# Hyena convolution: forward transform, spectral product and inverse transform in one phase

## The reference

```python
def long_conv_bidir(z, h_fwd, h_bwd):
    n = z.shape[1]
    nfft = 2 * n
    zf = jnp.fft.rfft(z.astype(jnp.float32), n=nfft, axis=1)
    hf = jnp.fft.rfft(h_fwd, n=nfft, axis=0) + jnp.conj(jnp.fft.rfft(h_bwd, n=nfft, axis=0))
    return jnp.fft.irfft(zf * hf[None], n=nfft, axis=1)[:, :n]

def hyena_branch(u, conv_w, conv_b, ...):
    x0, x1, v = jnp.split(short_conv(u, conv_w, conv_b), 3, axis=-1)
    z = x1 * v
    ...
    y = long_conv_bidir(z, h_fwd, h_bwd).astype(u.dtype) + z * skip
    return x0 * y
```

## Time and profile before

| what | value |
|---|---|
| median of 3 runs | 4414.9 us (4414.67 to 4422.24) |
| the profiled execution, its own time | 4423.86 us |
| its span in the trace | 4422.0 us |
| mean granted TensorE clock | 0.956 |
| TensorE busy | 3986.4 us (90%) |
| VectorE busy | 1482.3 us (34%) |
| ScalarE busy | 1015.8 us (23%) |

### The profile page before, as it was taken

How to read it: one execution, slowest core, us unless ns; L and a number is a source line. 1 busy time by engine, 2 the same in 40 slices (tenths; PEclk the granted TensorE clock), 3 DMA queues, 4 the chain that set the end, 5 groups by cost and what they waited for, 6 DMA issues and landing times. The chain is left out here.

```text
span 4422.0 us, 95422 instructions
## 1 busy us (share of the span) xinstructions
PE 3986.4 (90%) x41485; PEld 2616.3 (59%) x41485; DVE 1482.3 (34%) x2542; ACT 1015.8 (23%) x2416; POOL 606.4 (14%) x732
## 2 busy tenths in 40 slices
PE   7898799998999969999978999989999989997995
PEld 2343345885444458888854444459888944445774
DVE  2556321123212220000033666555666532222002
ACT  2200100022101112222233442034444311112433
POOL 1030000001110000000010001234555311000112
PEclk8899899999999979999989999989999999997998
DMA  6361211102111169999971001100000021124998
GB/s 218 114 206 63 109 45 67 38 10 53 50 33 60 65 234 393 398 401 395 393 270 41 7 5 43 39 6 4 4 3 4 4 89 49 51 91 182 389 383 317
DMA packets 233137, 588.67 MB, mean 133 GB/s; under 512 B 36424, under 2 KB 140776, under 8 KB 213193
## 3 DMA queue, kind: packets, MB, share of 16 engines
q1 hardware_dynamic: 192159, 462.92, 28.7%
q0 software_dynamic: 19120, 73.68, 4.8%
q10 hardware_dynamic: 21626, 48.70, 3.2%
HBM read 514.20 MB, written 71.05 MB: 132 GB/s over the span
## 5 line engine op out<-in xcount | busy, mean ns | idle before, releaser
L1646 PE MATMUL experts_bank<-experts_uT,ex_wu 128*64 128x96 f32 x9216 | 391.1, 247 | 26.9 <-PE experts_bank L1632 22.2
L1646 PEld LDWEIGHTS experts_bank<-experts_uT,ex_wu 128*64 128x64 f32 x9216 | 384.7, 138 | 43.6 <-issue 43.6
L1719 DVE TENSOR_TENSOR experts_hT<-experts_si,experts_bank 128x384 f32<-128x384 f32 (+1 forms) x68 | 31.3, 460 | 724.3 <-PE experts_bank L1646 724.3
L192 PE MATMUL vgproj_bank<-vg_w,mix_hT 128*128 128x256 f32 x1024 | 225.8, 383 | 11.1 <-DVEq L201 7.6
L192 PEld LDWEIGHTS vgproj_bank<-vg_w,mix_hT 128*128 128x128 f32 x1024 | 195.8, 192 | 41.5 <-DVEq L201 8.4
L1646 PE MATMUL experts_bank<-experts_uT,b2z_hT 128*64 128x96 f32 x4096 | 177.6, 248 | 27.3 <-DMA b2z_hT<-in_w 16.9
L1646 PEld LDWEIGHTS experts_bank<-experts_uT,b2z_hT 128*64 128x64 f32 x4096 | 172.1, 138 | 42.0 <-issue 42.0
L1632 PE MATMUL experts_bank<-mixed_T,experts_hT 128*32 128x256 f32 (+1 forms) x2592 | 193.9, 451 | 0.0
L2243 POOL TENSOR_TENSOR b2z_hT<-b2z_hT,rwkv_level 128x256 f32<-128x256 f32 x192 | 153.8, 834 | 159.4 <-DVE b2z_hT L2596 159.3
L2612 DVE TENSOR_TENSOR rc_xy<-rc_xy,rc_bank 128x256 f32<-128x256 f32 x288 | 120.7, 421 | 122.3 <-PE rc_bank L2257 116.6
L1632 PEld LDWEIGHTS experts_bank<-mixed_T,experts_hT 128*32 128x32 f32 x2592 | 110.4, 110 | 69.6 <-issue 0.2
(11 more groups left out here) (572 smaller groups left out, 7202.7 us busy)
## 6 DMA issues: line engine op xcount, KB each, us to landing
ex_wu<-in_expert_w SPq DMA_DIRECT2D x72, 2048.0 KB, 16.6
mixed_T<-in_expert_w SPq DMA_DIRECT2D x36, 2048.0 KB, 17.6
b2z_hT<-in_w SPq DMA_DIRECT2D x64, 1024.0 KB
b2z_Z<-in_w SPq DMA_DIRECT2D x32, 1024.0 KB, 13.6
keep_rows<-mix_hyT ACTq DMA_DIRECT2D x27, 768.0 KB, 8.9
keep_rows<-experts_yo ACTq DMA_DIRECT2D x68, 288.0 KB, 9.8
mix_hT<-in_ada_w POOLq DMA_DIRECT2D x8, 2048.0 KB, 10.0
merge_w<-in_w_in SPq DMA_DIRECT2D x32, 512.0 KB, 5.8
```

The source lines that it names most:

```text
L192: last = pe.matmul(bk[t][:, 0:width], xT[:, k, t * P:(t + 1) * P], wt[:, s, k, :], start=(k == 0), stop=(k == KT - 1))
L1646: last = pe.matmul(bk[2 + j][c:c + 64, h * BT:(h + 1) * BT], wu[:, s, j, k, h * P + c:h * P + c + 64], uT[:, s, k, :], start=(k == 0), sto ...
```

## The change

phase_forward and phase_inverse become one phase, phase_convolve. The forward part and the products stay instruction for instruction; two of the product's waits count differently (the semaphore turned takes one of the steps that chain counted, so chain counts four in a group).

The inverse matmuls are put into another order. Behind the forward matmuls TensorE issues, for par 0, the terms of the groups 0 to 2 (24 matmuls, first the four channel tiles of a = 0, then those of a = 1), which need only the first three products; then, when the fourth product is done, the last 8 terms of par 0; then par 1 as before, bank by bank. The inverse tables have no memory of their own any more: each comes as two halves of 1 MB. Those of par 0 go to the two halves of tab when the last two forward groups have been read from them, those of par 1 go to z and t when the fourth product is done. odd serves as the buffer of the closing VectorE instructions.

```diff
@@ -951,38 +951,71 @@
                     dve.tensor_tensor(H[:, kt, 3, :], odd[:, t % 2, :], even[:, :], ALU.subtract).then_inc(outs, 1)
 
 
-def phase_forward(nc, name, I, cos_in, sin_in, H, prod=None, y=None):
-
-
-    with Mem(nc, name) as m:
+def phase_convolve(nc, I, K, zn, H, prod, xc, hyT):
+
+
+    with Mem(nc, "conv") as m:
         tab = m.sb("tab", [P, 2, 16, P])
         odd = m.sb("odd", [P, 2, C])
-        z = m.sb("z", [P, 4, C]) if prod is not None else None
-        t = m.sb("t", [P, 4, C]) if prod is not None else None
+        z = m.sb("z", [P, 4, C])
+        t = m.sb("t", [P, 4, C])
+        y = hyT[:, :, 0:C]
+        back = [[tab[:, a, :, :].rearrange("p (k b) n -> p k (b n)", b=4) for a in range(2)], [z[:, :, :], t[:, :, :]]]
         bk = m.banks(8)
         full = m.sems("full0", "full1")
-        mm, free, copied, outs, chain = m.sems("mm", "free", "copied", "outs", "chain")
+        bfull = [m.sems("bfull00", "bfull01"), m.sems("bfull10", "bfull11")]
+        mm, copied, outs, chain, turned, bmm, skipped = m.sems("mm", "copied", "outs", "chain", "turned", "bmm", "skipped")
         b = m.block()
+        multiplied = lambda kt: 4 * (kt + 1)
 
         @b.sync
         def _(sp):
+            table = lambda par, a: I["k_inv"][par].rearrange("p (a n) -> p a n", n=C)[:, 4 * a:4 * a + 4, :]
             for kt in range(4):
                 if kt >= 2:
                     sp.wait_ge(mm, 4 * (kt - 1))
                 sp.dma_start(tab[:, kt % 2, :, :], I["k_fwd"][kt].rearrange("p (a n) -> p a n", n=P)).then_inc(full[kt % 2], 16)
+            for a in range(2):
+                sp.wait_ge(mm, 4 * (3 + a))
+                sp.dma_start(back[0][a], table(0, a)).then_inc(bfull[0][a], 16)
+            sp.wait_ge(chain, multiplied(3))
+            for a in range(2):
+                sp.dma_start(back[1][a], table(1, a)).then_inc(bfull[1][a], 16)
 
         @b.tensor
         def _(pe):
+
+            def inverse(par, c, a, kt, first, last):
+
+                return pe.matmul(bk[4 * par + c][:, :], prod[:, kt, 2 * par + a, c * P:(c + 1) * P], back[par][a][:, kt, :], start=first, stop=last)
+
             for kt in range(4):
                 pe.wait_ge(full[kt % 2], 16 * (kt // 2 + 1))
                 if kt >= 2:
                     pe.wait_ge(outs, kt - 1)
                 for a in range(4):
-                    src = cos_in if a < 2 else sin_in
                     for mt in range(4):
-                        last = pe.matmul(bk[kt % 2 * 4 + a][:, :], tab[:, kt % 2, a * 4 + mt, :], src[:, (a % 2) * 4 + mt, :],
+                        last = pe.matmul(bk[kt % 2 * 4 + a][:, :], tab[:, kt % 2, a * 4 + mt, :], zn[:, (a % 2) * 4 + mt, :],
                                          start=(mt == 0), stop=(mt == 3))
                     last.then_inc(mm, 1)
+            pe.wait_ge(outs, 3)
+            pe.wait_ge(chain, multiplied(2))
+            for a in range(2):
+                pe.wait_ge(bfull[0][a], 16)
+                for c in range(4):
+                    for kt in range(3):
+                        inverse(0, c, a, kt, a == 0 and kt == 0, False)
+            pe.wait_ge(chain, multiplied(3))
+            for c in range(4):
+                inverse(0, c, 0, 3, False, False)
+                inverse(0, c, 1, 3, False, True).then_inc(bmm, 1)
+            for a in range(2):
+                pe.wait_ge(bfull[1][a], 16)
+            pe.wait_ge(outs, 4)
+            for c in range(4):
+                for n in range(8):
+                    last = inverse(1, c, n // 4, n % 4, n == 0, n == 7)
+                last.then_inc(bmm, 1)
 
         @b.scalar
         def _(act):
@@ -997,15 +1030,12 @@
         def _(dve):
             then = Chain(dve, chain)
             for kt in range(4):
-                dst = [H[:, kt, n, :] for n in range(4)] if prod is None else [z[:, n, :] for n in range(4)]
                 dve.wait_ge(copied, 2 * kt + 2)
                 e = [bk[kt % 2 * 4], bk[kt % 2 * 4 + 2]]
-                dve.tensor_tensor(dst[0], e[0][:, :], odd[:, 0, :], ALU.add)
-                dve.tensor_tensor(dst[1], e[0][:, :], odd[:, 0, :], ALU.subtract)
-                dve.tensor_tensor(dst[2], odd[:, 1, :], e[1][:, :], ALU.add)
-                dve.tensor_tensor(dst[3], odd[:, 1, :], e[1][:, :], ALU.subtract).then_inc(outs, 1)
-                if prod is None:
-                    continue
+                dve.tensor_tensor(z[:, 0, :], e[0][:, :], odd[:, 0, :], ALU.add)
+                dve.tensor_tensor(z[:, 1, :], e[0][:, :], odd[:, 0, :], ALU.subtract)
+                dve.tensor_tensor(z[:, 2, :], odd[:, 1, :], e[1][:, :], ALU.add)
+                dve.tensor_tensor(z[:, 3, :], odd[:, 1, :], e[1][:, :], ALU.subtract).then_inc(outs, 1)
                 dve.wait_ge(outs, kt + 1)
                 h = [H[:, kt, n, :] for n in range(4)]
 
@@ -1015,12 +1045,25 @@
                     dve.tensor_tensor(t[:, 2, :], z[:, j, :], h[2 + j], ALU.mult)
                     then(dve.tensor_tensor(t[:, 3, :], z[:, 2 + j, :], h[j], ALU.mult))
                     dve.tensor_tensor(y[:, j, :], t[:, 0, :], t[:, 1, :], ALU.subtract)
-                    then(dve.tensor_tensor(y[:, 2 + j, :], t[:, 2, :], t[:, 3, :], ALU.add))
+                    last = dve.tensor_tensor(y[:, 2 + j, :], t[:, 2, :], t[:, 3, :], ALU.add)
+                    if j == 0:
+                        last.then_inc(turned, 1)
+                        dve.wait_ge(turned, kt + 1)
+                then(last)
 
                 dve.tensor_tensor(prod[:, kt, 0, :], y[:, 0, :], y[:, 1, :], ALU.add)
                 dve.tensor_tensor(prod[:, kt, 1, :], y[:, 2, :], y[:, 3, :], ALU.subtract)
                 dve.tensor_tensor(prod[:, kt, 2, :], y[:, 0, :], y[:, 1, :], ALU.subtract)
                 then(dve.tensor_tensor(prod[:, kt, 3, :], y[:, 2, :], y[:, 3, :], ALU.add))
+            split = lambda ap, par: ap.rearrange("p (n two) -> p two n", two=2)[:, par, :]
+            for par in range(2):
+                for c in range(4):
+                    n = par * 4 + c
+                    dve.wait_ge(bmm, n + 1)
+                    dve.scalar_tensor_tensor(odd[:, n % 2, :], split(xc[:, 4 + c, :], par), vec(K.cols, "hy_skip", c),
+                                             bk[n][:, :], ALU.mult, ALU.add).then_inc(skipped, 1)
+                    dve.wait_ge(skipped, n + 1)
+                    dve.tensor_tensor(split(hyT[:, c, :], par), odd[:, n % 2, :], split(xc[:, c, :], par), ALU.mult)
 
 
 def phase_hyena_turn(nc, K, xc, zn):
@@ -1046,45 +1089,6 @@
                     for c in range(4):
                         src = xc[:, 4 + c, :].rearrange("p (n two) -> p two n", two=2)[:, par, mt * P:(mt + 1) * P]
                         pe.transpose(bk[par * 4 + mt][:, c * P:(c + 1) * P], src, K.ident[:, :]).then_inc(tr, 1)
-
-
-def phase_inverse(nc, I, K, prod, xc, hyT):
...
 BIG = 1e30
@@ -3205,8 +3209,7 @@
         phase_taps(nc, "hin", w_in[:, :, 3072:4608], hT, K.X, xc, 6, lambda j, t: taps[j](t), col(b0), clear)
         zn = xc[:, 8:12, :].rearrange("p a (b c) -> p (a b) c", c=C)
         phase_hyena_turn(nc, K, xc, zn)
-        phase_forward(nc, "fwdz", I, zn, zn, H, prod, hyT[:, :, 0:C])
-        phase_inverse(nc, I, K, prod, xc, hyT)
+        phase_convolve(nc, I, K, zn, H, prod, xc, hyT)
 
 
 def moe(nc, tag, I, K, S, T, w_out, mixedT, wu, spare, mix_gate, hidden, scale, shift, run_cols, names, gate=None, ahead=None):
```

## The result

| | before | after |
|---|---|---|
| median | 4418.57 us (4 runs, 4414.67 to 4423.69) | 4395.61 us (4 runs, 4389.26 to 4400.4) |
| ratio to before, 95% interval | | 0.9945 (0.9933 to 0.9957) |
| profiled execution, its span | 4423.86, 4422.0 us | 4396.28, 4394.5 us |
| granted TensorE clock, mean | 0.956 | 0.958 |

The kernel is 0.55% faster; the forecast was 0.54% (4391.0, range 4386 to 4400). A ratio of 0.9945 on 4418.57 is 24.3 us; its interval, 0.9933 to 0.9957, is 19.0 to 29.6 us.

The account below looks back on a forecast made before the run. TensorE, busy 3986.4 of 4422.0 us, and its holes were taken as the bound. Forward end to inverse end falls from 79.01 to 54.93 + 0.2 = 55.13 us, saving 23.9: 4414.9 - 23.9 = 4391.0 us, range 4386 to 4400.

Parts of the forecast that it names:

- The three terms of the 24 us: Between forward and inverse transform: fourth product, barrier with table transfer, and low clock all vanish, saving 23.6 to 24.1 us.
- The marks set for the profile after: Signs expected in the new trace: no TensorE hole from 448 to 503, clock 1.00, next stage's first DMA at 505.9.
- The late weight load, 0.2 us: At TensorE's first inverse matmul, just after the third product: 0.2 us charged, bounds nothing to 0.5 us.
- The low clock, 2.0 to 2.2 us: At the old inverse's start, after TensorE's 21.9 us pause: 2.0 to 2.2 us lost, gone without a pause.
- The cover of 7.2 us: 24 inverse terms keep TensorE busy to 468.8; VectorE's fourth product is done 7.2 us before it is asked for.
- Charging nothing for the product beside a full TensorE: VectorE's fourth product beside inverse matmuls: same 0.68 to 0.69 us an instruction as beside an idle TensorE, no cost.
- The tables: SP's four 1 MB inverse table loads all hidden; margin 3 to 5 us for the second, at least 0.9 later.
- Rival B: Second table half lands 13.1 us after issue, TensorE stands: 3 to 5.4 us more, 4394 to 4396.5; chance 0.05.
- Rival C: TensorE still waits for the fourth product before the inverse: only 8.4 us saved, 4406.5; chance 0.03.
- Rival D: Short runs per bank in the inverse bring TensorE's low clock: slower, up to 4445.9 us; chance 0.02.
- Rival E: The following stage's first loads or a pause give back 3 to 16 us: 4394 to 4407; chance 0.06.

Follow-up runs that it names:

- e1: Changed kernel, but TensorE waits for the fourth product before its first inverse term, tables still early: 4409.32 us, ratio 0.9974 to the kernel before.
- e3: Changed kernel with TensorE waiting for the fourth product, and 15 useless matmuls filling that wait: 4411.78 us, ratio 0.9977 to the kernel before.
- e8: Changed kernel with par 0's second table half held back until the fourth product's second multiplication step: 4398.07 us, one execution.
- e5: Changed kernel with 18 useless VectorE instructions more in the fourth product: 4410.33 us, one execution.
- e2: Changed kernel in its new order, but par 0's two table halves asked for only after the fourth product: 4415.0 us, ratio 0.9984 to the kernel before.
- e4: Changed kernel with 8 useless VectorE instructions more in the fourth product: 4400.09 us, one execution.
- e6: Changed kernel with the loops of the first 24 inverse terms exchanged, another bank with every term: 4400.83 us, one execution.
- e7: Changed kernel with the first two forward tables loaded already in the phase before: 4392.63 us, ratio 0.9941 to the kernel before.
- e9: The changed kernel unedited, run once more on the chip of the early forward tables version: 4397.48 us, ratio 0.9947 to the kernel before.

## Why the prediction was right

- *The three terms of the 24 us.* The hole of 21.9 us and the low clock behind it were to vanish, 23.6 to 24.1 us together. The stage lost 24.00. The parts can be told apart by the experiments: waiting for the product costs 13.57 of pause (e1), the barrier and the transfer are the other 21.91 - 13.57 = 8.3 (by subtraction; no run puts back the barrier alone), and the low clock is separate from both (e3). The marks set for the profile after were met too, once the stage's later start of 1.6 us is taken off: the fourth product ended at 463.26 (461.6 forecast), the third table load was issued at 463.28 (461.7), the next phase's first load at 507.39 (505.9).
- *The late weight load, 0.2 us.* It was sized too high. The third product ends at 449.52, 0.27 us before the forward group's 449.79, and the first inverse group starts at 449.63 with no idle time. The whole inverse took 504.80 - 449.79 = 55.0 us against 54.93 + 0.2. Late weight loads can therefore have cost 0.1 us at most.
- *The low clock, 2.0 to 2.2 us.* Right for the kernel before. It isn't a constant: behind other pauses it was 1.6 (e8), 2.6 (e5, e1) and 3.06 us (e2), and not in the order of the pauses' lengths.
- *The cover of 7.2 us.* 5.8 us more on VectorE cost nothing, 13.0 us more made a pause of 5.9, that is 13.0 - 7.1 (e4, e5). Charging nothing for the product beside a full TensorE held too: it ran from 450.53 to 463.26, 12.73 us; before, beside an idle TensorE, it took 12.72.
- *The tables.* Four transfers, all hidden; those into z and t were issued at 463.28 and 463.65 and took 5.1 and 7.2 us to land, there by 470.9 and asked for at 477.2. (The prediction adds the second half's landing to 448.6 where it says that the half is free at 448.2; 0.4 us that change nothing.)
- *Rival B, a late table, 3 to 5.4 us.* The mechanism exists (e8); its price for a 4.6 us pause was 6.3 us. It didn't come about.
- *Rival C, no overlap, 8.4 us saved.* e1 is this case: 139.20 - 131.53 = 7.7 us saved in the stage. Most of the 0.7 us between is the low clock, 2.65 for 2.2.
- *Rival D, slower by the clock.* It fell in the changed kernel (clock 1.00 from 400 to 503) and in e6, where banks change with every term. But the prediction reads too much into the Trainium skill's section when it says that by that rule the rival would come about: what it tells of are pauses between groups, and TensorE had none here.
- *Rival E, given back later.* Nothing that the runs show to be due to the change: the next phase's first load comes as soon behind the last inverse matmul (507.39 - 504.80 = 2.59), as before (529.78 - 527.20 = 2.58). The 4.6 us between the median and the forecast aren't traced to a place. The kernel before had its median at 4418.57 with a fourth run, 3.7 us over the one the forecast started from, and the ratio of 0.9945 gives 24.3 us; so most of those 4.6 us lie in the reference value and in the scatter, not in the sum. That the median fell inside the range is thus partly a matter of which executions were timed; that the stage lost 24.0 us is not.

## What to carry to other kernels

When a hole in the bounding engine has two tenants one behind the other (a neighbour's last piece of work, then a transfer), both must move: hiding one alone left 16.4 or 22.0 of the 24 us in place. Look for terms of the next sum that don't need the last piece, issue them first, and let their table lie in memory that the phase has just finished with. Price a pause of TensorE of some 5 to 20 us by its length and 1.5 to 3 us of low clock behind it (one of 1.3 us, in e7, had none), and compare such small effects by a stage in the trace that both kernels have, since the whole time scatters by more.

## What the runs showed that was not expected

- **The same code takes different times outside the stage, and most of it is TensorE's pace.** Between the span's start and the first load of phase_forward_norm, which transforms the filters, lie 129.25 us in e2 and 137.16 us in e5, though nothing there was edited. These are the rows of SP's timeline, e2's first:

```profile
129.25 0.36 SPq L841 DMA_DIRECT2D fwdnorm_x<-in_x  x1
```

```profile
137.16 0.36 SPq L841 DMA_DIRECT2D fwdnorm_x<-in_x  x1
```

  The other nine profiles (before, after and the other runs) lie between these two values. The timelines of TensorE show where the 7.9 us go. Two groups of instructions in e2, and the busy times around the second:

```profile
37.71 1.92 PE L654 MATMUL front_bank<-mix_hT,front_cc 128*32 128x512 f32 x16
...
53.31 7.19 PE L683 MATMUL front_bank<-front_w,front_hid 64*128 64x512 f32 x8
```

```profile
53.00:63.00 10.00, 10.00 (x13) 3.94 (x14) 2.77 (x4) 3.96 (x5) 0.00 (x0) 0.50 0.93 349
```

  and the same in e5:

```profile
38.88 3.64 PE L654 MATMUL front_bank<-mix_hT,front_cc 128*32 128x512 f32 x16
...
60.51 7.19 PE L683 MATMUL front_bank<-front_w,front_hid 64*128 64x512 f32 x8
```

```profile
60.00:70.00 10.00, 10.00 (x14) 4.14 (x15) 2.77 (x4) 4.16 (x5) 0.00 (x0) 1.00 0.60 210
```

  The first group takes 1.92 us in e2 and 3.64 in e5; the second takes 7.19 in both. In e2 the granted clock beside that 7.19 is 0.50, in e5 it reads 1.00, for the same eight instructions in the same time. The smaller groups between them agree: those of L656 and L662 take 1.91 and 1.87 us in e5, as in e2 where its column reads 0.50, and 1.04 and 1.05 where it reads 1.00. So the clock column of e5 can't be right there: TensorE ran at the low pace from 33 to 71 us, with a column at 1.00. From the start of the first such group (32.84 in e2, 33.47 in e5) to that of the eight instructions (53.31 and 60.51) e5 falls back by 6.6 of the 7.9 us. Why it kept the low pace for so long stays open. The pace of instructions that two profiles share is the safer reading of the clock; where this text leans on a clock of 1.00 in the stage, the 0.429 us an instruction say the same. Beside this stand 17.8 us between the fastest and the slowest of the 11 timed runs of before in the last comparison (4411.4 to 4429.15), and 8.1 us between the eleven profiles in the part behind the stage (3885.4 in e3, 3893.5 in e6), which were not followed to their places.
- **A restart's cost depends on the execution.** Behind a pause of 5.95 to 6.45 us in ten of these profiles the forward group took 56.60 to 57.63 us, 1.5 to 2.5 over the 55.1 of the full clock; behind 1.27 us (e7) it took 55.17. Even a difference of one restart is as large as what an experiment here has to tell. The ten fall into two kinds by the 32 transposes of phase_hyena_turn that TensorE does just before that pause. The changed kernel's first profile and e9 show one of each:

```profile
380.60 5.26 PE L1091 MATMUL hturn_bank<-all_ident,hy_xc 128*128 128x128 f32 x32 [12.70 <-DVE hy_xc L1079]
```

```profile
379.16 6.50 PE L1091 MATMUL hturn_bank<-all_ident,hy_xc 128*128 128x128 f32 x32 [12.70 <-DVE hy_xc L1079]
```

  Where the transposes took 5.2 to 5.3 us (before, after, e1, e4, e6) the forward group took 57.56 to 57.63; where they took 6.2 to 6.7 (e2, e3, e5, e8, e9) it took 56.60 to 56.97. What one of the two saves the other pays, but for 0.8 us: their sum is 62.8 to 63.6 us in all ten. So the stage, which holds only the second, differs by up to 1 us between executions of one kernel, and a comparison should leave such a group out or take both in.
- **Useless matmuls win back only the low clock.** Filling a pause kept the clock at 1.00 and won 2.65 us (e3), by trace, of the 16.4 that the pause costs; no timed comparison here was fine enough to see it.
